# Column pieces through 20 buffers, tile 0's output product at the end of tile 1, side jobs from tile 2 on, scale summed in column halves

## The reference

```python
c_act = silu(c)
shift, scale, gate = split(c_act @ ada_w + ada_b, 3)         # 1024 x 3072 weights, one row
h = rmsnorm(x, norm_g) * (1 + scale) + shift
q, k, v, g_lr, r = split(h @ w_in)                           # 512, 512, 1024, 16, 1024 columns
log_a = log_sigmoid(g_lr @ w_alpha + b_alpha) / 16
o = chunked linear attention of q, k, v with decay exp(log_a), state carried over tokens
o = rmsnorm(o per head, norm_h) * silu(r)
x = rmsnorm(x + gate * (o @ w_out), final_g)
```

## Time and profile before

| | before |
|---|---|
| median of 3 runs | 2257.59 us (2256.69 to 2260.82) |
| profiled execution, time | 2259.05 us |
| its span, first to last instruction | 2256.9 us |
| outside the span | 2.15 us |
| mean granted TensorE clock (1 is 2.4 GHz) | 0.975 |
| PE, DVE, ACT, POOL busy over the span | 92%, 66%, 52%, 28% |

### The profile page before, as it was taken

One profiled execution on the slowest core, in us unless ns is written; L12 is line 12 of the kernel. 1 busy time (PEld: TensorE's weight loads), 2 busy tenths in 40 slices (PEclk: granted clock), 3 DMA queues, 4 the chain that ended last, 5 costly groups with the idle time before them and its releaser, 6 DMA issues. The chain is left out here.

```text
span 2256.9 us, 48556 instructions
## 1 busy us (share of the span) xinstructions
PE 2080.1 (92%) x19816; PEld 1446.8 (64%) x19816; DVE 1479.1 (66%) x2616; ACT 1178.4 (52%) x2561; POOL 623.8 (28%) x591
## 2 busy tenths in 40 slices
PE   4889999999999999499999999999995799999997
PEld 3536666666666666298999989989884334444342
DVE  7655555555555554267677777677774688888886
ACT  4634444444333443145454554455554688878885
POOL 3600010000000000243333444333433244444442
PEclk9989999999999999699999999999997899999999
DMA  8552222222222220801111001011103711121110
GB/s 321 179 164 87 81 86 83 77 77 92 82 87 94 90 83 29 268 21 31 28 32 46 28 27 32 27 38 39 28 18 118 223 65 49 57 66 38 38 38 29
DMA packets 140318, 174.57 MB, mean 77 GB/s; under 512 B 49088, under 2 KB 100416, under 8 KB 140096
## 3 DMA queue, kind: packets, MB, share of 16 engines
q1 hardware_dynamic: 139808, 170.42, 24.0%
q10 hardware_dynamic: 288, 1.05, 0.1%
HBM read 122.39 MB, written 49.03 MB: 76 GB/s over the span
## 5 line engine op out<-in xcount | busy, mean ns | idle before, releaser
L343 POOL TENSOR_TENSOR g_stage<-g_stage,g_nh_row 128x1024 f32<-128x1024 f32 x16 | 52.3, 3270 | 753.0 <-DVE g_stage L731 753.0
L2053 POOL TENSOR_TENSOR s_hi<-s_sp,s_cols 128x512 bf16<-128x512 f32 x144 | 163.1, 1133 | 301.2 <-DVE s_sp L2164 300.0
L1638 PE MATMUL m_bank<-h_hi,w_all 128*128 128x128 bf16 (+1 forms) x1280 | 218.5, 220 | 23.4 <-POOL m_arena L1229 19.8
L1638 PE MATMUL m_bank<-m_h_hi,w_all 128*128 128x128 bf16 (+1 forms) x1280 | 217.1, 219 | 3.9 <-DVE m_arena L1551 2.0
L1639 PE MATMUL m_bank<-h_lo,w_all 128*128 128x128 bf16 (+1 forms) x1280 | 218.2, 220 | 0.0
L1640 PE MATMUL m_bank<-h_hi,w_all 128*128 128x128 bf16 (+1 forms) x1280 | 218.1, 220 | 0.0
L1640 PE MATMUL m_bank<-m_h_hi,w_all 128*128 128x128 bf16 (+1 forms) x1280 | 216.8, 219 | 0.0
L1639 PE MATMUL m_bank<-m_h_lo,w_all 128*128 128x128 bf16 (+1 forms) x1280 | 216.8, 219 | 0.0
L824 PE MATMUL g_bank<-w_all,h_hi 128*128 128x512 bf16 x512 | 197.6, 386 | 14.2 <-ACT g_stage L462 7.0
L825 PE MATMUL g_bank<-w_all,h_hi 128*128 128x512 bf16 x512 | 197.2, 385 | 0.0
L826 PE MATMUL g_bank<-w_all,h_lo 128*128 128x512 bf16 x512 | 196.8, 384 | 0.0
(11 more groups left out here) (394 smaller groups left out, 6028.3 us busy)
## 6 DMA issues: line engine op xcount, KB each, us to landing
g_piece<-in_w_dram SPq DMA_DIRECT2D x64, 268.0 KB, 3.4
g_piece<-in_w_mod_t_dram SPq DMA_DIRECT2D x48, 256.0 KB, 3.2
w_hi<-g_piece_hi SPq DMA_DIRECT2D x64, 134.0 KB, 2.0
w_lo<-g_piece_lo SPq DMA_DIRECT2D x64, 134.0 KB, 2.2
g_xs<-in_x_dram SPq DMA_DIRECT2D x16, 512.0 KB, 3.9
g_stage<-in_ada_w_dram SPq DMA_DIRECT2D x16, 512.0 KB, 8.3
s_xr<-x SPq DMA_DIRECT2D x16, 512.0 KB, 4.2
out_dram<-s_xr SPq DMA_DIRECT2D x16, 512.0 KB, 2.6
```

Source lines behind the costliest of these rows:

```text
L343: pool.tensor_tensor(r_sb.rearrange("p (h e) -> p h e", h=GH), r_sb.rearrange("p (h e) -> p h e", h=GH), nh_row[:].unsqueeze(1).broadcast_ ...
L1638: pe.matmul(out, l_hi, r_hi, start=(k == 0), stop=False)
L2053: pool.tensor_tensor(hi[g % NH][:], sp_[k], one_col.broadcast_to([P, 512]), ALU.mult).then_inc(s["hi_done"], 1)
```

## The change

- Scale columns in halves. The shift columns still come as eight 512 KB DMAs, and the scale columns as 16 pieces of 512 columns (8 for each column half). Only the second half's loads wait for a slot. DVE sums 7 shift pieces and 16 scale pieces. The eighth shift piece goes through PE, multiplied by `c_act` straight from its slot. `modulation`, `h_make`, `h_high` and `h_low` of tile 0 run in halves; ACT instead of DVE scales `xn` for tile 0. `low_rank` starts on the first half of `h`. The `lo` of the low-rank columns and of Q piece 5 moves to POOL (6 on POOL, 3 on DVE), and DVE's three Q lows stand after `h_low`. The two memsets (`am`, `st[0]`) move from before tile 0 to behind `lows(2)`.
- 20 buffers for the 40 column pieces: the 8 old ones, 4 in `acc`, 8 in the Q columns' staging space. Piece j waits for the `lo` of piece j-20.
- `w_out` pieces: ACT's places for the highs are now 4 in tile 0, 4 after the statistics of O of tile 0, 4 after `og_high(0)` and 4 after V's first copy in tile 1. POOL takes the r gain of tile 0 after 4 lows rather than 8.
- Gate columns: their two accumulators are in `xo` and their two slots in `c2_row`; the loads are mixed into those of `w_out`. The 16 sums are spread over DVE's list as 3 and 2 in tile 0, then 2, 5 and 4 in tile 1.
- Tile 0's output product moves. PE does `sum_gate` (into banks O) and `y_products(0)` (into the KV banks) after `turn_x(2)` at the end of tile 1, and tile 1's keys-by-values product after its O. `og_lo` of tile 0 goes to `st[0]`. Tile 0's `x` is loaded a second time. `y_add`, `y_norm` and the store of tile 0 follow there.
- Side jobs begin in tile 2: 112 jobs over 13 tiles are 8 in tiles 2 to 6 and 9 in tiles 7 to 14. The silu of `c_2` moves from tile 1 to tile 2 on ACT, behind the second side job's high.

```diff
+        ring += [acc[:, n * 512:(n + 1) * 512] for n in range(4)]
+        ring += q_cols
+        NR = len(ring)
+        Q_POOL = (1, 3, 5, 6, 7)
+        Q_DVE = (0, 2, 4)
+        SHIFTS, SCALES = KB - 1, 2 * KB
         def side(i):
-            return range(PER_TILE * (i - 1), PER_TILE * i) if 0 < i < NT - 1 else range(0)
+            return range(first_side(i), first_side(i + 1)) if 1 < i < NT - 1 else range(0)
 # sync: loads
+            for kb in range(KB):
+                sp.dma_start(arena[:, kb * D:(kb + 1) * D], ada_w[0, kb * P:(kb + 1) * P, 0:D]).then_inc(slot_in[kb], 16)
             for n in range(2 * KB):
                 kb, half = n % KB, n // KB
-                wait("mod_acc", n - KB + 1)
+                if half:
+                    wait("mod_acc", kb // 2 + 1)
...
+            for half, kb in ((0, 0), (0, 1), (0, 2), (1, 0)):
+                load_gate(half, kb)
+            for r in range(KB):
+                load_wo(r)
+            sp.dma_start(xs[:, 0, :], x[0, 2 * T:3 * T, :]).then_inc(x_in[0], 16)
...
+            load_gate(0, 3)
+            load_gate(0, 4)
+            load_gate(0, 5)
+            load_gate(0, 6)
+            for r in range(KB, KB + 4):
+                load_wo(r)
+            load_gate(0, 7)
+            load_gate(1, 1)
+            for r in range(KB + 4, 2 * KB):
+                load_wo(r)
+            for kb in range(2, KB):
+                load_gate(1, kb)
+            wait("gate_done", 2 * KB)
+            sp.dma_start(x_first, x[0, 0:T, :]).then_inc(s["x0_in"], 16)
 # vector: start
+            for kb in range(SHIFTS):
+                dve.wait_ge(slot_in[kb], 16)
+                weighted_sum(acc[:, 0:D], arena[:, kb * D:(kb + 1) * D], kb, kb)
+            for n in range(SCALES):
+                kb, half = n % KB, n // KB
+                dve.wait_ge(scale_in[n], 16)
+                weighted_sum(acc[:, D + half * 512:D + (half + 1) * 512], scale_piece(n), kb, SHIFTS + n)
+            modulation(0)
+            h_make(0, halves=(0,))
+            modulation(1)
+            h_make(0, halves=(1,))
+            h_low_first(0)
+            h_low_first(1)
+            for kb in Q_DVE:
                 low(1 + kb, wi_hi[:, kb, Q0:Q0 + 512], q_cols[kb], wi_lo[:, kb, Q0:Q0 + 512])
 # tensor: tile(i)
                 by_token(G0[:], V0, "v_done")
-                if not first:
+                if i == 1:
+                    pe.wait_ge(s["og_lo_done"], 2)
+                elif i > 1:
                     y_products(i - 1)
-                if i == 1:
-                    sum_gate()
...
                 turn_x(i + 1)
+                if i == 1:
+                    pe.wait_ge(s["state_done"], 1)
+                    sum_gate()
+                    y_products(0)
+                    pe.wait_ge(s["gate_ready"], 2)
+                elif not last:
+                    keys_values(i)
```

More of the change, by code:

```diff
@@ L504, in tile @@
                 h_high(i + 1)
-                if first:
-                    wo_highs(4, KB)
                 act.wait_ge(s["r_used"], 2 * (i + 1))
@@ L623, in y_add, with y_add_first @@
                         pieces(between)
+            def y_add_first():
+                dve.wait_ge(s["x0_in"], 16)
+                dve.wait_ge(s["gate_ready"], 2)
+                for n, bank in enumerate((KV0, KV1)):
+                    half = slice(n * 512, (n + 1) * 512)
+                    dve.wait_ge(s["y_done"], n + 1)
+                    dve.tensor_tensor(xo[:, half], bank[:], gate_row[:, half], ALU.mult).then_inc(s["y_used"], 1)
+                    dve.wait_ge(s["y_used"], n + 1)
+                    dve.tensor_tensor(xo[:, half], xo[:, half], x_first[:, half], ALU.add).then_inc(s["x2_done"], 1)
             def y_norm(i):
@@ L688, in tile @@
                 if i == 1:
-                    gate_sums(1)
-                    gate_whole()
-                if i == 1:
-                    y_add(i - 1, 1 - par, range(0))
-                    pieces(side(i)[:5])
-                else:
+                    gate_sums(7, 12)
+                if i > 1:
                     pieces(side(i)[:2])
-                    if not first:
-                        y_add(i - 1, 1 - par, side(i)[2:3])
+                    y_add(i - 1, 1 - par, side(i)[2:3])
                     pieces(side(i)[3:5])
@@ L901, in low_rank, with keys_values @@
                 ins.then_inc(s["glr_done"], 1)
+            def keys_values(i):
+                pe.wait_ge(s["klT_copied"], i + 1)
+                wait("state_done", i)
+                for h in range(GH):
+                    ins = pe.matmul(KV[h // 2][:, (h % 2) * GDV:(h % 2 + 1) * GDV], klT[:, h * GDK:(h + 1) * GDK],
+                                    v_sb[:, h * GDV:(h + 1) * GDV], start=True, stop=True)
+                ins.then_inc(s["kv_done"], 1)
             def tile(i, par, first=False, last=False):
-                pe.wait_ge(s["h_lo_done"], i + 1)
                 wait("am_done", i)
                 if first:
-                    pe.wait_ge(s["w_lo_v"], 1)
-                low_rank()
+                    pe.wait_ge(s["w_lo_p"], 1)
+                low_rank(i)
                 pe.wait_ge(s["hf_done"], 2 * (i + 1))
@@ L930, in tile @@
                 by_token(G0[:], V0, "v_done")
-                if not first:
+                if i == 1:
+                    pe.wait_ge(s["og_lo_done"], 2)
+                elif i > 1:
                     y_products(i - 1)
-                if i == 1:
-                    sum_gate()
-                wait("y_used", 2 * i - 1)
+                    pe.wait_ge(s["y_used"], 2 * i - 1)
                 if first:
@@ L952, in tile @@
                 by_token(G0[:], R0, "r_done")
-                wait("y_used", 2 * i)
+                if i > 1:
+                    pe.wait_ge(s["y_used"], 2 * i)
                 pe.wait_ge(s["kl_scaled"], i + 1)
@@ L981, in tile @@
                 ins.then_inc(s["o_done"], 1)
+                if i == 1:
+                    pe.wait_ge(s["y_used"], 2)
+                    keys_values(i)
             turn_x(0)
@@ L1015 @@
 N_MOD = 2 * 3 * KB
-PER_TILE = 8
 N_SIDE = N_W2 + N_MOD
-assert N_SIDE == PER_TILE * (NT - 2)
 MASKED = -1e30
```

322 lines of the change are left out of this document (195 added, 127 removed).

## The result

| | before | forecast | after |
|---|---|---|---|
| median time, us | 2258.2 | 2225 (2216 to 2236) | 2238.8 (2235.7 to 2239.7) |
| span of the profiled execution | 2256.9 | 2224.2 | 2237.2 |
| first low-rank product | 38.15 | 35 | 35.30 |
| first Q product | 38.91 | 38.0 | 41.50 |
| last low on DVE ends | 79.4 | 75.2 | 82.6 |

The ratio of the times is 0.9907 (95% interval 0.9891 to 0.9923): 19.4 us or about 1% faster, in the direction forecast, 14 us short of it and outside the range. From the start of the last tile to the end of the span both take the same, 1401.0 and 1400.4 us, so the whole difference is made before, and nearly all of the shortfall lies in two rows: tile 1 starts 8.3 us later than forecast and takes 5.6 us longer.

A forecast was written before the change was run, and what follows sets the result against it. It took DVE's sums to bound the start and PE's own work from tile 2 on. Gains of 33.4 by tile 2's start and 0.9, less 1.6, take 32.7 us off the 2256.9 span: median 2225, range 2216 to 2236.

The forecast's parts named there:

- Tile 1's moves: Tile 1: PE's work reordered to cover its waits, taking 55.0 us instead of 83.07.
- the six waits: Tile 1 before the change: PE's six waits, 20.3 us together, each to be covered by the new order.
- The start: Before tile 0: DVE's sums end at 29.3, `h_low` at 35.0, Q's columns start at about 38.0 against 38.91.
- the pair price: Tile 0: a DVE low and a POOL low together cost about 1.6 us, so 20 pairs are 32 us.
- My sum: Tile 0, DVE's list: 35.0 + 36.1 busy + 2.9 Q lows + 1.2 wait = last low at 75.2.
- my first rival: Tile 0 gains nothing because DVE and POOL collide more: 2230, chance 0.20.
- a loss of 4: Tile 0's bound: every DVE low meets a POOL low, ten more cost 0.97 each, turning 5 us gain into none or this.
- 1.1 us allowed: Tile 1: allowance for thin covers, added to 53.9 to give 55.0.
- The covers: Tile 1: other work placed so that PE's six waits go; 53.9 us if each is covered.
- the last deadline of the gate chain: Tile 1: `sum_gate` due at 36.7 us, 16th gate sum at 37, so a wait of 0 to 1 us.
- The second rival: Tile 1: the gate chain is late, its 16th sum 6 to 8 us later: 2233, chance 0.17.
- The ninth jobs: Tiles 7 to 14: a ninth side job costs 0.2 us a tile, 1.6 in all, bounds 0 and 8.

The follow-up runs named there:

- Experiment 6: The kernel of experiment 3, now with all eight Q lows on DVE too: 2233.5 us, ratio 0.9894.
- experiment 3: Changed kernel with the lows of all forty column pieces on DVE: 2232.4 us, ratio 0.9884.
- experiment 4: Changed kernel with the loads of gate pieces (0,3) and (0,4) moved early on SP's queue, behind the first four w_out loads: 2234.7 us, ratio 0.9895.
- experiment 5: Changed kernel with gate loads (0,3), (0,4) early, plus tile 1's gate sums reordered and `sum_gate` between the output product's halves: 2233.5 us, ratio 0.9891.
- experiment 11: Changed kernel with old start, all column lows on DVE, early gate loads and reordered gate sums, plus ninth jobs in tiles 2 to 9: 2230.1 us.
- experiment 7: Changed kernel with the old start put back and eight buffers for the column pieces, keeping only the moves behind the start: 2237.5 us, ratio 0.9911.
- experiment 2: Changed kernel with the whole old start put back, twenty buffers and the rest of the change kept: 2233.6 us, ratio 0.9888.
- experiment 8: Changed kernel with old start, all forty column lows on DVE and gate loads (0,3), (0,4) early: 2228.8 us, ratio 0.9871.
- experiment 9: Changed kernel with old start, all column lows on DVE, early gate loads and the new order of gate sums: 2228.1 us, ratio 0.9869.
- 10: Changed kernel with old start, all column lows on DVE, early gate loads, reordered gate sums, and eight buffers instead of twenty: 2227.6 us, ratio 0.9866.

## Why the prediction was right in its direction and wrong in its size

**Tile 1's moves: right for four of the six waits.** The waits for the gate sums, the gate row, `h_low` and `g_glr` are gone, `sum_gate` is at the full clock, `y_products(0)` and the late `h_low` cover each other, tile 2 begins warm at 52.28. The silu of `c_2`, for which I put 0.4 us on the path, cost nothing.

**The start: the sums right, what follows wrong.** DVE's sums were to end at 29.3 and ended at 29.4; a half piece took 0.86 as forecast, the first of each half 0.68 and 0.58 instead of 0.57. The failed terms are what DVE does beside GpSimd: 1.8 us for the halves of `h_low` was 2.64, 2.9 for three Q lows was 4.76, and a step on 128x4 that I had counted at next to nothing was 1.13. Q started at 41.5, not 38.0. Experiment 6 takes GpSimd away and gets 1.47, 0.6 for each low, and 0.16.

**Tile 0: the pair price was right, and put on too few instructions.** My sum held that the list is as long as before, 36.1 us busy, plus three Q lows. I asked only whether *lows* would collide more, and they did not: 1.10 us each on average, after 1.16 before. The other steps of the list, from the gate's scan to `x_norm`, went up instead, and a collision costs most of them 0.8 to 1 us. DVE's busy time of 51.09 us against 40.16 is 2.1 for the lows (23 instead of 20), 1.6 for the half of `h_low` that now lies in the tile, 2.0 for gate sums, and 5.2 for longer operations of the rest.

Against my sum the last low ended at 82.6 instead of 75.2, 7.4 us late: `h_low` ended 1.7 later, the Q lows took 1.8 more, and the list behind them took 41.2 us instead of 37.3, 2.6 more busy and 1.3 more waiting. The other 0.9 us I put on the clock. I had R's second half start when the last low ends. It started at 83.47, not waiting for it but behind the first half, which had begun at 76.44 after three waits of PE (2.95, 2.65 and 1.62) and took 6.75 us instead of 5.35, in the stretch with a clock of 0.66 shown above.

I had the collisions as my first rival, with a chance of 0.20 and no gain in tile 0, and as a bound of "a loss of 4". Tile 0 didn't gain nothing, but lost 2.9 us at tile 1's start. The rival names a part of it. I had given the sentence of the Trainium skill (SBUF — State Buffer, "SBUF: two separate sides") that the two engines take the shared port pair in turn for a whole instruction. The runs bear it out beyond the lows, down to the step on 128x4 with 1.13 and 0.16 us; this step began at 29.66 and ended with the GpSimd operation beside it, at 30.8. Steps that read one tensor only, which my words didn't cover, were stretched as well: `x_norm` of 128x1024 took 1.64 us instead of 0.74, and the copy L791 on 128x8 1.12 instead of 0.17. That copy took 1.12 in tile 0 of the kernel before too, so the price for small steps could have been read there.

**Tile 1: 1.1 us allowed, 6.7 needed.** 53.9 was the plan without waits, and 60.62 came. The covers that failed are those of L462 (the copy of K) and L638 (`kl_scaled`). I had priced only the last deadline of the gate chain, `sum_gate`. It was kept, though the 16th sum ended 41.4 us into the tile and not at 37, since PE came to it only at 43.3. What failed is that each gate sum stands in DVE's list *in front of* something else. Sums 3 and 4 hold up the gate's first step, and so ACT and V's bank (1.8 us, experiment 4), sums 10 and 11 hold up `kl_scaled` (2.4 us, experiment 5; I had "due at 30 and ready at about 29.5"). With the second wait goes the clock, here from 125 to 136 us, in which R's second half took 7.03 us where the first had taken 5.35:

```profile
125.00:136.00 11.00, 8.63 (x35) 3.62 (x34) 6.36 (x12) 4.16 (x9) 2.37 (x3) 0.84 0.36 103
```

That is 2.4 + 1.8 + 1.7, and 0.3 for `sum_gate` over its 1.6: 6.2 of the 6.7. The second rival had the gate chain late, but at its end, where it wasn't.

**The ninth jobs: the sum right, the division wrong.** 0.2 us in each of eight tiles was 1.8 in tile 7 and nothing in the others. In tile 7 the sixth and seventh job are both splits:

```profile
456.60 1.33 DVE L655 TENSOR_TENSOR g_piece_lo<-g_piece,g_piece_hi 128x536 bf16<-128x536 f32 x2
462.53 0.69 DVE L661 SCALAR_TENSOR_TENSOR g_piece<-g_piece,w_all 128x512 f32<-128x512 f32 x1 [4.59 <-DMA g_piece<-in_w_mod_t_dram]
...
465.12 0.72 DVE L655 TENSOR_TENSOR g_piece_lo<-g_piece,g_piece_hi 128x536 bf16<-128x536 f32 x1 [1.90 <-ACT g_piece_hi L473]
465.76 2.64 DVE L646 TENSOR_SCALAR g_xn<-g_bank,g_cols 128x128 f32<-128x128 f32 x8
...
470.89 0.24 PE L1025 MATMUL g_bank<-h_hi,w_all 128*32 128x128 bf16 x4 [1.73 <-DVE h_lo L680]
```

SP has two of their four stores ahead of the eighth job's load and the other two ahead of the ninth's:

```profile
457.33 0.33 SPq L329 DMA_DIRECT2D w_hi<-g_piece_hi  x1
457.70 1.54 SPq L330 DMA_DIRECT2D w_lo<-g_piece_lo  x1
459.29 0.43 SPq L321 DMA_DIRECT2D g_piece<-in_w_mod_t_dram  x1
459.76 0.45 SPq L329 DMA_DIRECT2D w_hi<-g_piece_hi  x1
460.26 0.43 SPq L330 DMA_DIRECT2D w_lo<-g_piece_lo  x1
460.73 0.48 SPq L318 DMA_DIRECT2D g_piece<-in_w_dram  x1
```

The ninth job ends at 465.8, some 2 us after `h_make` was due (463.6, by its place in the tile of the earlier trace rows). That another division of the jobs moves the cost is shown by experiment 11; that the stores are what does it was only read from the trace. Why tile 7 takes 52.93 to 53.28 us with the old start and 54.07 to 54.54 with the new stays open.

**The shortfall in numbers.** At tile 1's start 8.3 us are missing. By runs, with the edits taken in this order:

| | tile 1 starts | forecast | measured |
|---|---|---|---|
| kernel before | 91.86 | | |
| the moves alone (experiment 7) | 94.11 | 0 | 2.2 later |
| and twenty buffers (experiment 2) | 92.95 | 5.1 earlier | 1.2 earlier |
| and the new start (the change) | 94.79 | 0.2 earlier | 1.8 later |

The forecast's 5.1 are 4.0 us of DVE's waits in the list (41.3 less 36.1 less 1.2) and 1.1 between its last low and R's second half; its 0.2 are 3.1 less 2.9. So about 4 us of the missing 8.3 are on the buffers and 2 each on the start and on the moves, which I had put at nothing in tile 0; each to 1 or 2 us, as single executions go. All column lows on DVE and the old start, with the early gate loads, give 7.0 of the 8.3 back (94.79 to 87.81, experiment 8). Of the 5.6 us in tile 1 experiment 5 gives 5.2 (60.62 to 55.44). No kernel has all of it at once: with all four edits (experiment 9) the profiled last tile starts at 825.78 and the time is 2228.1, 30 us faster than before. Experiments 8, 9 and 10 beat both kernels and can't be told apart.

## What to carry to other kernels

When a change feeds two engines better that share something, count as colliding every instruction of the busier one in that stretch, not only the kind that is moved; here the second engine's help cost more than it gave. When work with loads of its own is spread through an engine's list, price what stands behind each piece, not only the last deadline. And keep the parts of a change apart in the measurement: this one gained 20 us by its moves and some 3 by its buffers, and its new start lost 4 to 5 of it.

## What the runs showed of the hardware that I had not expected

- Forty lows on one engine at 0.68 us are faster than twenty each on two at 1.10 and more: tile 1 starts at 89.67 instead of 94.79.
- A DVE step on 128x4 takes 0.16 us alone and 1.13 beside a GpSimd operation, and a copy of one tensor on 128x8 0.17 and 1.12.
- A short wait of PE can cost about as much again in the clock behind it: Q's products 7.16 us instead of 5.53 after 2.1 us of waiting, and R's first half 6.81 or 5.13 after the same 2.5, by the clock granted in that execution. What decides between the two isn't shown.
